# Weight sums of two up-projections made ahead in DRAM by adding transfers, PSUM banks by longest unused, rows kept in float32, and the eight early pairs in a row

## What is computed

```
y  = mixed @ w_out
x  = x + gain * rmsnorm(y)               # the residual
h  = rmsnorm(x) * gain (+ shift)
u  = dwconv(h @ w_up) + bias             # 1024 x 5632, three taps
x  = x + gain * rmsnorm((val * act(gate)) @ w_down)      # val, gate = halves of u
```

## Time and profile before

| | |
|---|---|
| median of 3 runs | 3728.32 us (3721.13 to 3732.64) |
| the profiled execution | 3724.28 us, of which its span 3722.4 us |
| PE / DVE / ACT busy | 3406.6 / 2404.7 / 1582.8 us |
| late part of mixer 1, from the first P6 | about 1495.8 to 1970 us of the span |
| late part of mixer 2 | about 2956 to 3431 us of the span |

### The profile page before, as it was taken

The page is one execution under the profiler, slowest core; times in us unless marked ns, Lnnn a source line. Parts: engine busy times, 40 slices in busy tenths (PEclk is TensorE's granted clock), DMA queues, the critical chain, the costliest instruction groups (busy, mean ns, idle before and its releaser), DMA issues.

```text
span 3722.4 us, 73022 instructions
## 1 busy us (share of the span) xinstructions
PE 3406.6 (92%) x30711; PEld 3081.6 (83%) x30711; DVE 2404.7 (65%) x3809; ACT 1582.8 (43%) x2735; POOL 182.5 (5%) x335
## 2 busy tenths in 40 slices
PE   7999999999989897788898999999999788898999
PEld 4787789888877775666668999899999788898999
DVE  5477778878757746777776884322235777777565
ACT  4556644444347634333334553111134333334454
POOL 2000000000000010000000111000000000000110
PEclk9999999999889999899999999999999899999999
DMA  6234442323233052222325763111123222232774
GB/s 241 71 128 139 140 163 97 112 92 96 55 74 87 1 162 87 63 68 79 95 69 192 262 216 122 29 35 46 49 85 117 80 70 84 69 91 84 261 239 159
DMA packets 328479, 410.36 MB, mean 110 GB/s; under 512 B 15795, under 2 KB 255894, under 8 KB 328152
## 3 DMA queue, kind: packets, MB, share of 16 engines
q1 hardware_dynamic: 298184, 306.49, 26.9%
q0 software_dynamic: 29968, 99.19, 8.2%
HBM read 322.68 MB, written 82.94 MB: 109 GB/s over the span
## 4 chain that ended last, share of the span: by engine, by line
PE 38%; DVE 14%; issue 4%; DVEq 3%; ACT 3%; DMA 2%; ACTq 0%; POOL 0%
PE psum L3586 5%; PE psum L3588 4%; PE psum L3587 4%; PE psum L2846 4%; PE psum L2847 4%; PE psum L2848 4%; PE psum L2369 3%; PE psum L2371 3%; PE psum L2370 3%; DVE mix_u_val L3870 3%; DVE mix_u_gate L3870 2%; DMA down_w_raw<-in_w_down 2%; DVE mix_w_split L3407 2%; ACT mix_w_split L3402 2%; PE psum L2705 1%
## 5 line engine op out<-in xcount | busy, mean ns | idle before, releaser
L2235 DVE TENSOR_TENSOR down_w_lo<-down_w_raw,down_w_hi 128x1024 fp32r<-128x1024 f32 x228 | 270.5, 1186 | 442.2 <-ACT down_w_hi L2209 440.1
L3586 PE MATMUL psum<-mix_t_hi,mix_w_split 128*128 128x258 f32 (+1 forms) x1056 | 358.2, 339 | 145.6 <-DVE mix_x_gate L3858 86.2
L2209 ACT ACTIVATE down_w_hi<-down_w_raw 128x1024 fp32r<-128x1024 f32 x228 | 234.6, 1029 | 572.0 <-PE psum L2848 328.4
L2369 PE MATMUL psum<-down_ghi,down_w_hi 128*128 128x256 f32 x1408 | 404.5, 287 | 12.4 <-DVE down_glo L2240 12.2
L2371 PE MATMUL psum<-down_glo,down_w_hi 128*128 128x256 f32 x1408 | 399.7, 284 | 0.0
L2370 PE MATMUL psum<-down_ghi,down_w_lo 128*128 128x256 f32 x1408 | 399.5, 284 | 0.0
L3586 PEld LDWEIGHTS psum<-mix_t_hi,mix_w_split 128*128 128x128 f32 x1056 | 211.0, 200 | 180.7 <-DVE mix_w_split L3407 106.1
L3587 PE MATMUL psum<-mix_t_hi,mix_w_split 128*128 128x258 f32 (+1 forms) x1056 | 351.2, 333 | 0.0
L3588 PE MATMUL psum<-mix_t_lo,mix_w_split 128*128 128x258 f32 (+1 forms) x1056 | 350.8, 332 | 0.0
L3407 DVE TENSOR_TENSOR mix_w_split<-mix_w_raw,mix_w_split 128x512 fp32r<-128x512 f32 x240 | 165.1, 689 | 212.2 <-ACT mix_w_split L3402 211.9
L2369 PEld LDWEIGHTS psum<-down_ghi,down_w_hi 128*128 128x128 f32 x1408 | 271.6, 193 | 14.5 <-DVE down_glo L2240 14.1
(11 more groups left out here) (501 smaller groups left out, 8676.5 us busy)
## 6 DMA issues: line engine op xcount, KB each, us to landing
down_w_raw<-in_w_down SPq DMA_DIRECT2D x176, 512.0 KB, 4.3
mix_w_raw<-in_w_up SPq DMA_DIRECT2D x104, 512.0 KB, 5.3
g_scratch<-mix_u_val POOLq DMA_DIRECT2D x44, 512.0 KB, 4.0
down_w_raw<-in_w_in SPq DMA_DIRECT2D x36, 512.0 KB, 4.0
down_g_part<-g_scratch POOLq DMA_DIRECT2D x6, 2816.0 KB, 17.2
rw_operands<-step_set SPq DMA_DIRECT2D x16, 1024.0 KB, 6.4
mod_w<-in_w_mod POOLq DMA_DIRECT2D x32, 512.0 KB, 5.6
mix_w_raw<-in_w_out SPq DMA_DIRECT2D x32, 512.0 KB, 4.0
```

The lines of the kernel that those rows point to most:

```text
L2209: self.nc.scalar.activation(self.hi[s][:, 0:w], self.raw[s][:, 0:w], ACT.Copy).then_inc(self.w_high, 1)
L2235: last = self.nc.vector.tensor_tensor(self.lo[s][:, 0:w], self.raw[s][:, 0:w], self.hi[s][:, 0:w].bitcast(F32), ALU.subtract)
L2369: nc.tensor.matmul(out, w_hi[:, w], g_hi[:, :], start=(n == 0 and c % 2 == 0), stop=False, skip_group_check=True)
L3586: nc.tensor.matmul(out, w[:, 0, c], xh[:, x], start=(first and kk == 0), stop=False, skip_group_check=True)
```

## The change

It makes the four combinations of `w_up` ahead of their use, in new DRAM tensors `up_sums` (4 x 512 x 2816 for each mixer). For each mixer POOL issues 32 transfers of 128 rows by 2816 columns: 16 copies from DRAM to DRAM and then 16 that add their source to what lies in DRAM. For mixer 1 one stands behind each of the 32 `mod_w` loads of the scan, for mixer 2 all stand at the end of `down1`'s POOL queue, ahead of its wait for the stage. The fifth to eighth rounds (index 16 and on) wait for earlier transfers. The four sums on DVE go; SP loads one tile of 256 KB for every step into ten buffers and waits once in each mixer, ahead of the loads of the late part, for the sums.

The rows of h and of b11 and b21 are kept in float32 where t1 and t4 will be made (`final`), so that `add_turns` has four DVE operations in place of six. For a = 1 the chain starts its residuals two at a time and ends sooner: means at e = 8, scaled rows at 10 and 11, `add_turns` at 11 to 14, and the splits of t3, t1, t4 and b22 are spread over e = 15 and the first four late steps. EARLY is 0 to 7, so the first eight pairs of the late part have five steps and the other 14 have seven. A product goes to the PSUM slot (one bank in mixer 1, two in mixer 2) that was unused longest.

```diff
@@ scan, POOL: for i in range(4 * KD)
                 pool.dma_start(k.mod_w[i % 3][:, :], w_mod[:, kk, c:c + MOD_COLS]).then_inc(mod_landed[i % 3], 16)
+                sum_weights(pool, k, 0, i)
@@ down1.gpsimd, after the tables
+        for i in range(32):
+            sum_weights(pool, self.k, 1, i)
         pool.wait_ge(self.used, self.total)
@@
-EARLY = [3, 5, 7, 9, 0, 1, 11, 13]
+EARLY = list(range(8))
-FIRST_ROWS = 14
+FIRST_ROWS = 8
+def sum_weights(pool, k, mixer, at):
+    j, c = divmod(at, 4)
+    w, active_first = ((k.ins["w_up"][0], False), (k.ins["w_up_2"][0], True))[mixer]
+    val, gate = (slice(FF, 2 * FF), slice(0, FF)) if active_first else (slice(0, FF), slice(FF, 2 * FF))
+    sums, done, base = k.up_sums[mixer], k.sums_done[c], 128 * mixer
+    low, high = slice(P * c, P * c + P), slice(512 + P * c, 512 + P * c + P)
+    if j < 4:
+        src = (w[low, gate], w[low, val], w[low, val], w[high, val])[j]
+        pool.dma_start(sums[j, low, :], src).then_inc(done, 16)
+    elif j < 6:
+        src = (w[high, gate], w[low, gate])[j - 4]
+        pool.wait_ge(done, base + 64)
+        pool.dma_start(sums[(0, 2)[j - 4], low, :], src, accum_op=ALU.add, max_dma_last_dim=5632).then_inc(done, 16)
+    else:
+        pool.wait_ge(done, base + 16 * j)
+        pool.dma_start(sums[(1, 3)[j - 6], low, :], sums[(0, 1)[j - 6], low, :],
+                       accum_op=ALU.add, max_dma_last_dim=5632).then_inc(done, 16)
@@ banks: for each late step
+        if kind in ("P2", "P3"):
+            slot = slot_of["P1" if kind == "P2" else "P5", i]
+        else:
+            slot = min(range(SLOTS), key=lambda j: last_use[j])
+            freed_by[kind, i] = user.get(slot)
...
+        last_use[slot] = STEPS if kind in ("P1", "P5") else s
@@ weight_low: the four sums on DVE go (add_weights, and the sum ahead of P4)
-        if s + 1 < STEPS and s + 1 >= first_late:
-            kind, i = steps[s + 1]
-            if kind == "P6":
-                add_weights(dve, i)
...
@@ sync
+        for s in range(STEPS):
+            if s >= RAWS:
+                sp.wait_ge(*w_low.at(s - RAWS + 1))
...
+            if s == first_late:
+                for done in k.sums_done:
+                    sp.wait_ge(done, 128 + 128 * spec["mixer"])
+            sp.dma_start(raw[s % RAWS][:, :].rearrange("p (k n) -> p k n", n=P), source(s)).then_inc(w_landed[s % RAWS].sem, 16)
@@ add_turns
-            tt(f["t1"], h0[0][kk][:, :].bitcast(F32), b12, ALU.subtract)
+            tt(f["t1"], f["t1"], b12, ALU.subtract)
             tt(f["t3"], b12, b22_row, ALU.subtract)
-            dve.drain()
-            tt(f["t1"], f["t1"], h0[1][kk][:, :].bitcast(F32), ALU.add)
             dve.drain()
             tt(f["t2"], b22_row, f["t1"], ALU.add).then_inc(t_added.sem, 1)
             dve.drain()
-            tt(f["t4"], h0[0][kk + 4][:, :].bitcast(F32), f["t2"], ALU.subtract)
-            dve.drain()
-            tt(f["t4"], f["t4"], h0[1][kk + 4][:, :].bitcast(F32), ALU.add).then_inc(t4_added.sem, 1)
+            tt(f["t4"], f["t4"], f["t2"], ALU.subtract).then_inc(t4_added.sem, 1)
@@ DVE, chain(a, e)
+            elif a == 1:
+                if 3 <= e <= 6:
+                    residual(a, 2 * e - 6, 2 * e - 5)
+                elif e == 8:
+                    means(a, 1)
+                elif e in (10, 11):
+                    scale_rows(a, 4 * e - 40)
+                    if e == 11:
+                        add_turns(0)
+                elif 12 <= e <= 14:
+                    add_turns(e - 11)
+                elif e == 15:
+                    low_turns("t2")
@@ DVE, late steps
-            if s in (first_late, first_late + 1):
-                low_turns(TURNS[3 + s - first_late])
+            if first_late <= s < first_late + 4:
+                low_turns(TURNS[1 + s - first_late])
```

More of the change, by code:

```diff
@@ L3232, in vector @@
             self.finish_rows(dve, self.last, half)
-EARLY = [3, 5, 7, 9, 0, 1, 11, 13]
+EARLY = list(range(8))
 QUEUE = len(EARLY)
 KEPT = {i: j for j, i in enumerate(EARLY + [i for i in range(KF) if i not in EARLY])}
-X_BUFFER = [6, 7] + [i // 2 - 1 if i % 2 and i < 14 else 6 + i % 2 for i in range(2, KF)]
-FIRST_ROWS = 14
+X_BUFFER = [i if i < 8 else 6 + i % 2 for i in range(KF)]
+FIRST_ROWS = 8
 def half_groups(n):
@@ L3294, in mixer_out_to_ffn @@
     h0, b22, turn, turn_f32 = spec["h0"], spec["b22"], spec["turn"], spec["turn_f32"]
-    ring, raw, tmp = spec["ring"], spec["raw"], spec["tmp"]
+    ring, raw = spec["ring"], spec["raw"]
+    final = lambda a, kk: y[1][:, kk, :] if a else turn_f32["t4" if kk >= 4 else "t1"][kk % 4][:, :]
     w_out = spec["w_out"].rearrange("(k p) n -> p k n", p=P)
     w_up = spec["w_up"].rearrange("(k p) n -> p k n", p=P)
+    w_sums = [k.up_sums[spec["mixer"]][j].rearrange("(k p) n -> p k n", p=P) for j in range(4)]
     UNITS = 2 * KD
@@ L3320, in mixer_out_to_ffn @@
     xv = lambda i: stash[X_BUFFER[i]]
-    fresh = [i for i in range(KF) if i not in EARLY]
-    kept_before = lambda i: max([QUEUE] + [KEPT[j] + 1 for j in fresh if j <= i - SETS])
     low_cols, high_cols = slice(dst, dst + n), slice(dst + n, dst + 2 * n)
@@ L3428, in sync @@
-    def sync(sp):
-        for r in range(TILES):
-            if r >= 4:
-                sp.wait_ge(*w_low.at(released[r - 4]))
-            elif before and r < 2:
-                sp.wait_ge(before.low, before.total - 1 + r)
+        nc.vector.tensor_tensor(ring[s % 4][:, 1, :], raw[s % RAWS][:, :], ring[s % 4][:, 0, :].bitcast(F32),
+                                ALU.subtract).then_inc(w_low.sem, 1)
+    def sync(sp):
+        for s in range(STEPS):
+            if s >= RAWS:
+                sp.wait_ge(*w_low.at(s - RAWS + 1))
+            elif before and s < 4:
+                sp.wait_ge(before.low, before.total - 1 + s // 2)
@@ L3569, in tensor @@
             a, e = chain_of(s)
-            first = kind in ("P1", "P6", "P7", "P5") or (kind == "O" and steps[s][2] == 0)
+            first = kind not in ("P2", "P3") and (kind != "O" or steps[s][2] == 0)
             for j in range(nb):
@@ L3574, in tensor @@
                 else:
[L3575 removed]
+                    out = k.psum[:, late_bank(i, kind, j), 0:pw]
                 if kind == "P2":
@@ L3826, in chain @@
                 scale_rows(a, 4)
-                if a == 0:
-                    low_rows(0)
-                else:
-                    add_turns(0)
+                low_rows(0)
             elif e == 15:
-                if a == 0:
-                    low_rows(4)
-                else:
-                    for kk in range(1, 4):
-                        add_turns(kk)
-                    for which in TURNS[0:3]:
-                        low_turns(which)
+                low_rows(4)
         def take(s):
@@ L3959, in mixer_memory @@
     h0 = [[first_rows[:, kk // 4, q, kk % 4, :] for kk in range(KD)] for q in range(2)]
-    spots = iter(spots)
+    first_spots, later_spots = iter(first_spots), iter(later_spots)
     turn, turn_f32 = {}, {}
-    for which in ("t1", "t2", "t3", "t4", "b22"):
-        places = [[next(spots) for _ in range(4)] for _ in range(2)]
+    for which in ("t1", "t4", "t2", "t3", "b22"):
+        lasting = which in ("t1", "t4")
+        places = [[next(first_spots if lasting and q else later_spots) for _ in range(4)] for q in range(2)]
         turn[which] = [four_tiles(k, f"{name}_{which}_{p}", n, places[q], F32R) for q, p in enumerate(("hi", "lo"))]
```

208 lines of the change are left out of this document (94 added, 114 removed).

## The result

The changed kernel takes 3816.73 us (median of 4 runs, 3811.66 to 3824.06) where the kernel before, run beside it, takes 3730.48 us (3721.13 to 3735.48): a ratio of 1.0236, 95% interval 1.0207 to 1.0265. It is 2.4% slower. The forecast was 3593 us, 3.6% faster, so the prediction is wrong in sign and far outside its range.

The account below looks back on a forecast made before the run. It took the kernel as PE-bound stages with holes where DVE is late in the mixers' late parts. 107 (sums off DVE) + 37 (head) - 9 = 135 us less gave 3589, by median 3593 us; range 3550 to 3660.

Parts of the forecast that it names:

- Pairs of five at 17.8 us: Late part of each mixer: without its sums DVE needs 17.8 us a pair, was 19.94; these pairs stay DVE-bound.
- Pairs of seven at 19.6 and 19.75 us: Late part: these pairs become PE-bound, 19.6 us in mixer 1 and 19.75 in mixer 2, where they took 22.50.
- The head: Start of each mixer's late part: 18.4 us gained, 37 in both, with 9 set against it.
- The 135 us gained in the tails: Whole forecast gain: 107 from sums leaving DVE, plus 37 from the head, minus 9.
- "Cost nothing": New bank rule in the mixers: a late take no longer stops PE at once; no time of its own.
- "The transfers": Scan and stage behind down1: sums moved to DMA, 12.6 us an addition, would cost 0; 185 us at 25.8.
- 302 us fit into 480: Behind down1: mixer 2's 16 copies at 6.3 and 16 additions at 12.6 us end before POOL's x loads.
- that limit, 13.5 us an addition: Scan: the last mod_w load lands in time while an addition takes no more than 13.5 us; above, DVE waits.
- the fifth rival: Scan and 2284 to 2764 us: SP's weight loads suffer, some 30 by 3 us beyond cover, 90 us, 3683; chance 0.03.
- The prediction's own sign of being wrong: Wrong if, among other signs, the stages from 480 to 1300 us or from 2284 to 2764 us grow.
- The fourth: Scan: additions above 13.5 us hold up mod_w, up to 3778 us; chance 0.05 beyond 22.5 us, 0.08 for 14 to 22.
- The chance of 0.05 for slower: Whole kernel: chance of measuring slower, beside 0.92 for faster and 0.03 for the same.

Follow-up runs that it names:

- e8: The changed kernel with the fixed PSUM banks of the kernel before, transfers and all else unchanged: 3842.92 us, ratio 1.0304 to the kernel before.
- e10: Changed kernel, mixer 1's sums divided: 8 in scan behind unit loads, 24 in attention, two in flight; mixer 2's one in flight, behind loads: 3592.55 us.
- e1: The changed kernel without any sum transfers, plain tiles of w_up loaded in place of sums: 3588.25 us, ratio 0.9617 to the kernel before.
- e3: The changed kernel with only mixer 2's sum transfers (behind down1), mixer 1 loading plain tiles of w_up: 3701.74 us, ratio 0.9922 to the kernel before.
- e5: The changed kernel with POOL waiting for each sum transfer to land before issuing the next: 3628.91 us, ratio 0.9743 to the kernel before.
- e6: The changed kernel with one sum transfer in flight, each issued only once a load of SP's has landed: 3611.63 us, ratio 0.9689 to the kernel before.
- e4: The changed kernel with its 32 adding transfers made as plain copies of the same source and place: 3784.37 us, ratio 1.015 to the kernel before.
- e7: The changed kernel with one transfer in flight and mixer 1's 32 sums moved from the scan to the attention stage: 3653.88 us, ratio 0.9806.

## Why the prediction was wrong

**What held.** DVE's 130 us less: 129. Pairs of five at 17.8 us: 17.6. Pairs of seven at 19.6 and 19.75 us: 19.60 and 20.07. First to last tap 399 and 401 us: 396.3 and 404.6. PE's wait before the first P6 some 6 us: 7.3 and 5.9. The head, 37 - 9 = 28 us in both mixers: from the first x load to the first val tap it is 18.8 us less in mixer 1 and 10.2 in mixer 2. The 135 us gained in the tails: 139.3 by the cuts, and 3588 us without the transfers for the 3593 forecast. "Cost nothing" for the banks holds for the new rule, and e8 shows the 23 to 26 us that the old one would have cost. The reason given, that "the pace of 19.6 us needs" it, does not hold: with the old banks the pairs of seven keep 19.60 us, and the pairs of five, which the prediction had bound by DVE alone, slow down.

**The step that failed** is the part "The transfers", where it goes through the two places in which they lie, and it failed in both: it put at nothing what the transfers do to SP's loads beside them. The runs show 111.5 us behind down1 and 124.3 us in the scan.

Behind down1 it read "PE is covered by weights loaded two jobs ahead; a load that takes some 10 us longer reaches nobody". As far as the runs go the cover is there: in e10 a weight load took up to 9.9 us to land, 6 us over the 4.0 of before, and the stretch stayed at 482.8 us. The 10 us were the error: no row gave them. Sixteen transfers issued at once are a queue of 88 us, and the loads issued beside it and the additions behind it took 33.6 to 77.6 us. The sum had priced the queue for the transfers' own end (302 us fit into 480) and never for a load that comes in beside it.

In the scan it asked only whether `mod_w` lands in time behind the additions, and set that limit, 13.5 us an addition. It never bound: DVE didn't wait for `mod_w`. The unit loads were left out of the sum. Their cover was in the trace of before, 556.00 to 562.19 us, and wasn't looked up; the fifth rival said "cover of some 20 us, two jobs" for them too, which was read from the other stage. (It is also this fifth rival, and not the last, that prices the turns between queues.) With 6 us of cover and landings of 5.5 us there was nothing to spare: the median landing came 10 us later, ACT waited 189 us in all, and 124 us, two thirds of it, come out on the span. The prediction's own sign of being wrong, that these two stages grow, was the right one to watch.

**The rivals.** The fifth had the mechanism and the side (loads of SP beside the sums, 3683 us, chance 0.03), with 30 loads by 3 us beyond cover. Measured were 18 waits of 10.5 us in the scan and 112.7 us in 4 waits of ACT behind down1. It was mis-sized by a factor of 2.6 (235.8 for 90) and its chance was far too low, because its "against" rested on the borrowed cover. The fourth, slow additions, had the larger chance and the wrong victim. The chance of 0.05 for slower should have been that of a change which nearly doubles POOL's DMA bytes (191 MB for 99), all in two stretches, with a row for the cover of the loads in neither.

**What is shown and what is argued.** e1 to e3 show that the sums' transfers cost the two stretches their length. Behind down1 it is shown that neither their bytes as such nor their adding do it: with the same transfers one at a time (e5) all but 2 of the 111.5 us are gone. In the scan the same wait gives back 82 of 124 us, holding the sums behind the unit's loads (e6) 10 more, and additions made as plain copies (e4) alone 30, so there the length of a transfer counts as well. Whether a load waits for the depth of the queue or for engines that are full is not separated: e5's wait lowered both, the share of the DMA engines from 1.00 to 0.74. That the rest in the scan (22 us of e6 against e7) is PE's own instructions coming late over the same DMA engines is argued: PE's waits for nothing shown are 26.0 us in e6 and 6.7 in e7, but no run changed the instructions, and other runs with 32 sums have 15.9 and 17.2. The Trainium skill, page "Runtime: NRT & Kernel Launch", section "Instruction fetch mechanics", says that an engine fetches its instructions through a DMA queue of its own while it works and that this is mostly hidden. The first half would allow such waits beside the sums. If they are of that kind, the second holds for e10's 8 sums (4.9 us) and not for e6's 32 (26.0 us).

## What to carry to other kernels

Work that moves onto the DMA engines is priced by what it does to each load that is issued while it is queued. For every such load look up its cover, from issue to first use, in the trace, stage by stage; the mean DMA share of before and the transfers' own end didn't show it here. Where bulk transfers must lie beside loads, let their issuer wait for each to land and start them behind the loads with the least cover: here that, with most of mixer 1's sums moved to attention, was worth 224 us (e10) with the same bytes moved in all.

## What the hardware showed

- A 512 KB load issued beside the queued DRAM-to-DRAM transfers of 1408 KB (16 copies, then additions) took up to 77.6 us to land (median 53.6), without them 4.0 us, and beside one transfer at a time 5.3 us.
- Copies of 1408 KB from DRAM to DRAM took 5.5 us each when 16 were queued; in attention they came every 6 to 12 us one at a time (e7) and every 5.2 to 6.5 us with two in flight (e10, from its third issue there on). The last eight additions behind down1, some four of them in flight, came every 7.4 us, and plain copies in their place (e4) every 4.8 us; one at a time an addition came every 10 us. The prediction cites the Trainium skill, page "Collectives: The Full Stack", section "Part 3: Why 7× under link rate", for half the rate of a copy. These transfers don't bear that out: 7.4 for 4.8 us is 1.5 times.
- The adding itself took nothing from PE behind down1: 598.7 us with plain copies for 594.3 with additions. In the scan it took 30 us.
